# Hybrid attention and mixture-of-experts block on one core: projections as three rounded products, moved within the attention steps, and twenty products of constants in the head

## Chip, cores and metric

The kernel runs on one core of one Trainium2 chip. The metric is the device time of one execution in microseconds. The core has TensorE (PE, with its own queue of weight loads, PEld), VectorE (DVE), ScalarE (ACT), GpSimd (POOL) and the sequencer SyncE (SP), which only issues transfers here.

## What is computed

One decoder layer over 512 tokens of width 1024, all in float32. Cut to what matters here:

```python
mod = silu(c) @ w_ada + b_ada                 # six vectors: shift, scale, gate for attention and for ffn
h = rms_norm(x, g_attn) * (1 + scale_a) + shift_a
proj = h @ w_in                               # 3072 columns: dq dk dv | sq sk sv, 512 each
a_out = diff_attention(rms_norm(dq), rms_norm(dk), dv)     # 4 heads, two 64-wide maps each, ALiBi
b_out = stick_breaking_attention(sq, sk, sv)               # 8 heads of 64
x = x + gate_a * (concat(a_out, b_out) @ w_out)
h = rms_norm(x, g_ffn) * (1 + scale_f) + shift_f
x = x + gate_f * hier_moe(h)                  # best of 4 groups, best 2 of 8 experts in it, 32 experts
```

## The kernel before

The kernel is written by hand, one program per engine, with semaphores between them; within an engine the order is the program order, so a wait holds back all that stands behind it on that engine.

**Head.** SP loads x (2 MB), eight quarters of the shift and scale columns of w_ada (1 MB each) and then the first of six pieces of w_in (2 MB each, 512 columns; two places in the tile `stage`, so piece n is loaded once the last job of piece n-2 is done). ACT normalizes x, PE transposes it, DVE sums the w_ada quarters weighted with silu(c) (`first_sums`, line 799), PE adds the sums over partitions (`column_sums`, line 1242), DVE makes `mod`, and ACT writes hT, the modulated transposed input, in eight tiles k (line 590). POOL loads both gate biases (1 MB together, line 496), and from the middle of the scale sums on the remaining w_ada quarters (line 514).

**Projection jobs.** `plan_jobs` numbers the jobs: qk 0 to 7 (dq, dk), v 0 to 3 (dv), two gate jobs, then sq 0 to 3, sk 0 to 3, and four jobs v(n,1) (sv), with two `col` jobs (sums over partitions for the shift and scale of the ffn), `shift_router` and two more gate jobs among them. Job n writes PSUM bank n % 2 and waits until job n-2's result was read out. A job has eight k. The jobs qk 1 to 7 and v 0 to 3 run in `run_split`: weight and input are each split into a rounded part (hi) and a rest (lo), and three products of type float32r stand for one float32 product (line 1333). For them ACT rounds a chunk of 128 weight columns (`w_round`, line 598), DVE subtracts (`w_rest`, line 846), and hT is split the same way (lines 850, 853 on DVE, 506 on POOL). The other projection jobs run in `run` as float32 products (lines 1280 and 1285), which PE carries out as two instructions each. While the qk jobs run, ACT and DVE also norm dq and dk (lines 612 to 620, 874).

**Attention steps.** The loop over s runs on PE, ACT and DVE. Step s < 16 belongs to unit s (head s // 4, row block s % 4, width 128 to 512 columns). On PE before the change: `scores(s)` (line 1355), `probT_make(s-1)` (transposes, line 1369), `pv(s-2)` (line 1381), sometimes `fin_T` (line 1391), and last the projection parts of the step: two halves in steps 0 to 7, one in steps 8 to 15. On ACT: read out the jobs of step s-1, copy the transposes of unit s-1 (`probT_evac(s-1)`, line 661), exponentials of unit s (`exp_unit(s)`, line 653). On DVE: read out jobs of step s-1, `combine_unit(s-1)` (lines 934 to 938), `max_unit(s)` (lines 923, 927), then in steps 0 to 7 one w_ada quarter (lines 798, 799).

```python
for s in range(STEPS):                        # ACT, before
    if 1 <= s < DIFF_STEPS:
        for job in step_jobs.get(s - 1, ()):
            job_evac(job)
    if 1 <= s <= NT * DH:
        probT_evac(s - 1)
    if s < NT * DH:
        exp_unit(s)
```

Steps 16 on are stick-breaking attention, then the output projection (line 1474), routing, and 16 pairs of experts (lines 1582, 1601) whose 96 MB of weights SP loads into slots as they come free; the tiles hT, qkT, mixT, alibi, obuf, stage and val serve as those slots.

Of the kernel before, what the change touches and what calls it, by code (L numbers as in the profile page):

```python
# [5 lines left out]
F32 = mybir.dt.float32  # L6
# [7 lines left out]
P = 128  # L14
# [55 lines left out]


# [31 lines left out]
def hymba_block(nc, x, c, w_ada, b_ada, g_attn, w_in, q_norm_g, k_norm_g, lambda_q1, lambda_k1,  # L103
# [11 lines left out]
    with ExitStack() as ctx:  # L115
# [18 lines left out]
        xr = sb("xr", [P, NT, D])  # L134
        stage = placed_sb("stage", [P, 3, 4096])
        hT = sb("hT", [P, KD, T])
        qkT = placed_sb("qkT", [P, 16, T])
        val = sb("val", [P, NT, 1024])
        mixT = placed_sb("mixT", [P, KD, T])
# [3 lines left out]
        obuf = placed_sb("obuf", [P, 4, T])  # L143
# [13 lines left out]
        hT_hi = rounded("hT_hi", [P, KD, T], "qkT", 8 * T)  # L157
        hT_lo_parts = [rounded("hT_lo0", [P, 4, T], "mixT"), rounded("hT_lo1", [P, 4, T], "obuf")]
# [3 lines left out]
        def hT_lo(k):  # L162
            return hT_lo_parts[k // 4][:, k % 4, :]
# [88 lines left out]
        wr_ready = sem("wr_ready")  # L252
# [98 lines left out]

        def split_chunk(n):
# [4 lines left out]
            return raw[:, :, part], w_hi[:, :, part], lo[:, :, part], arrived, value  # L357
# [10 lines left out]
        def _(sp):  # L368
# [40 lines left out]
            sp.wait_ge(job_done, job_no[("v", 3, 1)] + 1)  # L409
            sp.wait_ge(ada_used, 16)  # L410
# [41 lines left out]
        def _(pool):  # L452
# [42 lines left out]
            for n, v in enumerate((GATE_A, GATE_F)):  # L495
                g.dma_start(gates[:, n, :], row(b_ada[:, v * D:(v + 1) * D])).then_inc(gate_bias_in, 16)

            for v in range(GATE_A, GATE_F + 1):
                for i in range(4):
                    n, dst, arrived, _ = quarter(v, i)  # L500
                    if n == 0:
                        pool.wait_ge(scale_used, KD // 2)
                    if n == 2:
                        for k in range(1, KD, 2):
                            pool.wait_ge(hT_hi_ready, k + 1)
                            g.tensor_tensor(hT_lo(k), hT[:, k, :], hT_hi[:, k, :].bitcast(F32),
# [7 lines left out]
                    g.dma_start(dst, ada_v[:, 2 * i:2 * i + 2, v * D:(v + 1) * D]).then_inc(arrived, 16)  # L514

            for w in range(2 * NT - 1):
# [46 lines left out]
        def _(act):  # L563
# [1098 lines left out]
```

## Time and profile before

| | us |
|---|---|
| median of 3 runs | 682.06 |
| lowest, highest | 679.41, 684.06 |
| profiled execution | 682.16 |
| its span, first to last instruction | 680.0 |
| PE busy in it | 561.3 (83%) |
| DVE, ACT, POOL busy | 275.7, 170.2, 82.2 |
| mean granted TensorE clock | 0.938 |

All rows below are of the profiled execution and start at its first instruction. "L1280 x16" means sixteen instructions of line 1280. A matmul's recorded duration overlaps the next one's; the distance from one start to the next is what it costs. In the chain of waits each piece is what the following one waited for.

### The profile page before, as it was taken

The numbers are of one execution on the slowest core, as the hardware profiler recorded it, in microseconds if no ns is written. First come the engines' busy times: TensorE is split into PE (matmuls) and PEld (weight loads), VectorE is DVE, ScalarE is ACT, GpSimd is POOL, SyncE is SP. The second block draws the span as 40 slices with busy tenths as digits, with TensorE's granted clock in tenths as the row PEclk, the third lists the DMA queues.
The fourth block names the chain that finished last, engine by engine and source line by source line (L and its number), as shares of the span: only waits on it lengthen the run. The fifth ranks groups of instructions, "written<-read, shape, count | busy, mean of one in ns | idle before, by whom it ended". The sixth has DMA issues, their size and how long they took to land.

```text
span 680.0 us, 7324 instructions
## 1 busy us (share of the span) xinstructions
PE 561.3 (83%) x2832; PEld 330.4 (49%) x2832; DVE 275.7 (41%) x474; ACT 170.2 (25%) x310; POOL 82.2 (12%) x98
## 2 busy tenths in 40 slices
PE   3379989999989899999999925988998898788740
PEld 2347768446455445665445613544554454344410
DVE  3866680553734455655012275222322232222005
ACT  7045541221222336786133210000000000000002
POOL 8331100000000000000021202111121112010000
PEclk9999999997998899999999955999999999889985
DMA  8984753537120007000751382899999999999719
GB/s 344 407 271 168 276 211 134 185 124 247 62 92 33 1 0 308 2 0 1 293 232 62 129 335 70 319 417 416 416 416 417 415 417 417 418 417 417 315 42 355
DMA packets 42384, 163.24 MB, mean 240 GB/s; under 512 B 7796, under 2 KB 7796, under 8 KB 34164
## 3 DMA queue, kind: packets, MB, share of 16 engines
q1 hardware_dynamic: 31972, 134.52, 49.6%
q0 software_dynamic: 9248, 26.23, 10.9%
q10 hardware_dynamic: 1136, 2.11, 0.8%
q8 instruction: 19, 0.31, 0.2%
q14 instruction: 9, 0.07, 0.0%
HBM read 158.64 MB, written 12.58 MB: 252 GB/s over the span
## 4 chain that ended last, share of the span: by engine, by line
PE 67%; DMA 14%; SPq 7%; DVE 7%; ACT 3%; issue 2%; POOLq 0%; DVEq 0%; ACTq 0%
PE banks L1582 11%; PE banks L1280 10%; PE banks L1474 8%; PE banks L1333 8%; PE banks L1601 6%; PE banks L1285 4%; DMA stage<-in_w_in_dram 4%; DMA stage<-in_w_dram 4%; DMA qkT<-in_w_dram 4%; PE banks L1426 3%; PE banks L1410 2%; PE banks L1570 2%; DMA stage<-pair_rows 2%; SPq L371 2%; PE banks L1355 1%
## 5 line engine op out<-in xcount | busy, mean ns | idle before, releaser
L1601 PE MATMUL banks<-stage,work 128*64 128x512 f32 x168 | 63.1, 638 | 10.0 <-ACT work L767 5.8
L1280 PE MATMUL banks<-hT,stage 128*128 128x512 f32 x144 | 66.4, 616 | 1.5 <-DMA stage<-in_w_in_dram 1.5
L1582 PE MATMUL banks<-qkT,work 128*64 128x256 f32 x272 | 63.6, 391 | 0.0
L765 ACT ACTIVATE work<-banks 128x256 f32<-128x256 f32 x16 | 6.1, 384 | 222.6 <-PE banks L1582 222.6
L1474 PE MATMUL banks<-stage,mixT 128*128 128x512 f32 x128 | 56.2, 594 | 0.0
L1185 DVE TENSOR_TENSOR work<-banks,gates 128x1024 f32<-128x1024 f32 x16 | 19.6, 1225 | 85.5 <-PE banks L1601 85.5
L1582 PE MATMUL banks<-hT,work 128*64 128x256 f32 x192 | 45.2, 394 | 2.6 <-DMA qkT<-in_w_dram 2.6
L799 DVE SCALAR_TENSOR_TENSOR mixT<-stage,small,mixT 128x1024 f32<-128x1024 f32 x35 | 44.9, 1282 | 3.5 <-DMA stage<-in_w_ada_dram 2.8
L1280 PEld LDWEIGHTS banks<-hT,stage 128*128 128x128 f32 x144 | 27.9, 199 | 34.0 <-issue 31.5
L1180 DVE TENSOR_TENSOR work<-work,banks 128x256 f32<-128x256 f32 x16 | 6.7, 421 | 88.3 <-ACT work L765 88.3
L534 POOL DMA_INDIRECT pair_rows<-work,tables x16 | 16.1, 1005 | 202.4 <-DVE work L1185 202.4
L1582 PEld LDWEIGHTS banks<-qkT,work 128*64 128x64 f32 x272 | 37.1, 140 | 5.9 <-issue 0.8
L1582 PE MATMUL banks<-mixT,work 128*64 128x256 f32 x160 | 36.0, 381 | 3.5 <-DMA obuf<-in_w_dram 2.4
L1474 PEld LDWEIGHTS banks<-stage,mixT 128*128 128x128 f32 x128 | 24.0, 190 | 28.9 <-issue 28.9
L1582 PE MATMUL banks<-stage,work 128*64 128x256 f32 x160 | 35.8, 381 | 0.0
L1582 PEld LDWEIGHTS banks<-hT,work 128*64 128x64 f32 x192 | 26.6, 142 | 18.9 <-issue 4.8
L1601 PEld LDWEIGHTS banks<-stage,work 128*64 128x64 f32 x168 | 17.9, 146 | 34.3 <-issue 28.0
L519 POOL TENSOR_TENSOR xr<-xr,obuf 128x512 f32<-128x512 f32 x7 | 8.8, 1266 | 191.1 <-DVE obuf L1023 191.1
L1285 PE MATMUL banks<-stage,hT 128*128 128x512 f32 x64 | 31.2, 634 | 0.0
L1582 PEld LDWEIGHTS banks<-mixT,work 128*64 128x64 f32 x160 | 21.3, 137 | 15.1 <-DMA obuf<-in_w_dram 3.3
L923 DVE CUSTOM_DVE_ANT_0 work<-banks,alibi 128x128 f32<-128x128 f32 (+3 forms) x32 | 14.4, 488 | 32.8 <-PE banks L1355 32.8
L514 POOL DMA_DIRECT2D stage<-in_w_ada_dram x16 | 11.5, 721 | 122.1 <-DVE mixT L799 122.1
(263 smaller groups left out, 1089.4 us busy)
## 6 DMA issues: line engine op xcount, KB each, us to landing
stage<-in_w_dram SPq DMA_DIRECT2D x31, 1024.0 KB, 20.5
qkT<-in_w_dram SPq DMA_DIRECT2D x23, 1024.0 KB, 20.9
stage<-in_w_ada_dram POOLq DMA_DIRECT2D x16, 1024.0 KB, 5.6
stage<-in_w_in_dram SPq DMA_DIRECT2D x6, 2048.0 KB, 10.1
hT<-in_w_dram SPq DMA_DIRECT2D x12, 1024.0 KB, 18.2
val<-in_w_dram SPq DMA_DIRECT2D x10, 1024.0 KB, 18.4
mixT<-in_w_dram SPq DMA_DIRECT2D x10, 1024.0 KB, 18.6
alibi<-in_w_dram SPq DMA_DIRECT2D x5, 1024.0 KB, 23.6
```

The costliest lines, as they stand in the source:

```text
L371: sp.dma_start(dst[i // 2][:, 2 * (i % 2):2 * (i % 2) + 2, :], ada_v[:, 2 * i:2 * i + 2, v * D:(v + 1) * D]).then_inc(first_in[4 * v + i], 16)
L534: g.indirect_dma_start(y_dram, bass.IndirectOffsetOnAxis(ap=tables[:, 1, q:q + 1], axis=0), ysb[:, r, :], None, bounds_check=2 * T - 1, oo ...
L799: return v.scalar_tensor_tensor(out=dst, in0=src, scalar=s, in1=dst, op0=ALU.mult, op1=ALU.add)
L923: ins = v.tensor_tensor_reduce(out=prob[:, u % 2, m, 0:W], in0=banks[:, 2 + 2 * (u % 2) + m, 0:W], in1=alibi[:, h, T - W:T], scale=1.0, sc ...
L1185: v.tensor_tensor(ysb[:, r, :], banks[:, 4 + 2 * r:6 + 2 * r, :].rearrange("p b k -> p (b k)"), gates[:, 1, :], ALU.mult).then_inc(ysb_rea ...
L1280: ins = mm(bank, w[:, k, ch * P:(ch + 1) * P], hT[:, k, :], start=(k == 0), stop=(k == KD - 1))
L1285: ins = mm(bank, hT[:, k, job[1] * P:(job[1] + 1) * P], w[:, k, :], start=(k == 0), stop=(k == KD - 1))
L1333: ins = mm(bank, still, moving, start=(k + m == 0), stop=(k == KD - 1 and m == 2))
L1426: ins = mm(zps[n % 2][:, o:o + W], still[:], part[:, n % 2, ZOFF[j]:ZOFF[j] + W], start=False, stop=True, skip_group_check=True)
L1474: ins = mm(banks[:, w % 5, :], mixT[:, k, t * P:(t + 1) * P], wv[:, k % 4, half * 512:(half + 1) * 512], start=(k == 0), stop=(k == KD - 1))
L1582: ins = mm(banks[half * C:(half + 1) * C, 2, up * F:(up + 1) * F], heT[:, r, k * P + half * C:k * P + (half + 1) * C], ws[2 * place + half ...
L1601: ins = mm(banks[half * C:(half + 1) * C, 4 + 2 * r + col, :], geT[:, fc * P + half * C:fc * P + (half + 1) * C], w2s[2 * place + half][:, ...
```

## The change

- All twelve float32 projection jobs and job qk 0 now run as three float32r products. ACT and DVE split chunks 12 to 23 of w_in for them: chunk 12 behind the head, chunk s+13 in step s up to step 5, then 19 and 20, 21 and 22, 23 in steps 6, 7 and 8. In each step this stands last, behind `exp_unit(s)` on ACT and behind the w_ada quarter on DVE.
- POOL splits chunk 0. Job qk 0 first makes its products with the rounded input, then those with the rest.
- The rounded input lies over x, whose tile is loaded again (2 MB) after the last projection; the rest lies over hT itself. DVE writes all eight rounded tiles before its four rests.
- The gate jobs of the head stand before v 0 to 3, no longer behind them. POOL's w_ada quarters also wait for piece 0 of w_in, and each gate bias is loaded behind its own quarters.
- On PE the projection parts of a step stand directly behind `scores(s)`, before `probT_make(s-1)`. Step 8 has no projection part, step 15 two; `col` 3 and `shift_router` are in step 8, the two late gate jobs in steps 12 and 14. The second eight w_ada quarters are summed in steps 0, 2, 4, 6, 8, 9, 10, 11.
- Before the column sums of the scale, once its last quarter is in, PE runs twenty bf16 products of constants (128x256) into an unused part of a bank.

```diff
-    head = [("qk", n) for n in range(8)] + [("v", t, 0) for t in range(NT)] + [("gate", 0, 0), ("gate", 0, 1)]
+    head = [("qk", n) for n in range(8)] + [("gate", 0, 0), ("gate", 0, 1)] + [("v", t, 0) for t in range(NT)]
...
-        for _ in range(2 if s < 8 else 1):
+        for _ in range({8: 0, 15: 2}.get(s, 2 if s < 8 else 1)):
             steps[s].append(halves.pop(0))
     steps[3].append((("col", 2), None))
-    steps[7].append((("col", 3), None))
-    steps[9] += [(("gate", 1, 0), None), (("shift_router",), None)]
-    steps[11].append((("gate", 1, 1), None))
+    steps[8] += [(("col", 3), None), (("shift_router",), None)]
+    steps[12].append((("gate", 1, 0), None))
+    steps[14].append((("gate", 1, 1), None))
...
+ADA_STEPS = (0, 2, 4, 6, 8, 9, 10, 11)
...
+        hT_hi = rounded("hT_hi", [P, KD, T], "xr")
+        hT_lo = rounded("hT_lo", [P, KD, T], "hT")
+        w_hi_spare = rounded("w_hi_spare", [P, KD, P], "work", 3072)
...
+        def split_at(s):
+            return {0: (13,), 6: (19, 20), 7: (21, 22), 8: (23,)}.get(s, (s + 13,) if s < 6 else ())
...
             sp.wait_ge(job_done, job_no[("v", 3, 1)] + 1)
+            sp.dma_start(xr[:], x_rows).then_inc(x_again, 16)
...
-            for n, v in enumerate((GATE_A, GATE_F)):
-                g.dma_start(gates[:, n, :], row(b_ada[:, v * D:(v + 1) * D])).then_inc(gate_bias_in, 16)
+            raw, hi, lo, arrived, value = split_chunk(0)
+            pool.wait_ge(arrived, value)
+            g.tensor_copy(hi, raw).then_inc(w0_hi, 1)
+            pool.wait_ge(w0_hi, 1)
+            g.tensor_tensor(lo, raw, hi.bitcast(F32), ALU.subtract).then_inc(w0_split, 1)
...
                     if n == 0:
                         pool.wait_ge(scale_used, KD // 2)
+                        pool.wait_ge(piece_in[0], 16)
...
                 act.wait_ge(arrived, value)
-                if n >= 4:
-                    act.wait_ge(job_done, n - 3)
+                if hi_before(n) is not None:
+                    act.wait_ge(job_done, job_no[chunk_job(hi_before(n))] + 1)
+                if n == 12:
+                    act.wait_ge(norm_done, 8)
                 a.activation(hi, raw, ACT.Copy).then_inc(w_hi_ready, 1)
...
             for job in head_jobs:
                 job_evac(job)
+            w_round(12)
...
                 if s < NT * DH:
                     exp_unit(s)
+                for n in split_at(s):
+                    w_round(n)
...
             for job in head_jobs:
                 job_evac(job)
+            w_rest(12)
...
-                if s < 8:
-                    ada_quarter(SCALE_F + s // 4, s % 4)
+                if s in ADA_STEPS:
+                    i = ADA_STEPS.index(s)
+                    ada_quarter(SCALE_F + i // 4, i % 4)
+                for n in split_at(s):
+                    w_rest(n)
...
             column_sums(0, shift_used)
+            pe.wait_ge(first_in[7], 16)
+            for _ in range(20):
+                mm(banks[:, 0, 256:512], ident_bf, consts[:, 5, :].bitcast(BF16), start=False, stop=True,
+                   skip_group_check=True)
             column_sums(1, scale_used).then_inc(col_a, 1)
...
+            def project(job, bank, ks):
+                c = IN_JOBS.index(job)
+                lo = w_lo_parts[:, c // 4 % 2, :].rearrange("p (k n) -> p k n", k=KD)
+                if job[0] == "v":
+                    pe.wait_ge(w_split, c // 4 * 4 + 3)
...
+                if c == 0:
+                    pe.wait_ge(w0_split, 1)
+                    for k in ks:
+                        pe.wait_ge(hT_hi_ready, k + 1)
+                        mm(bank, w_hi[:, k, part], hT_hi[:, k, :], start=(k == 0), stop=False)
+                        mm(bank, lo[:, k, part], hT_hi[:, k, :], start=False, stop=False)
                     pe.wait_ge(hT_lo_dve, KD // 2)
                     pe.wait_ge(hT_lo_pool, KD // 2)
+                    for k in ks:
+                        ins = mm(bank, w_hi[:, k, part], hT_lo[:, k, :], start=False, stop=(k == KD - 1))
+                    return ins
+                pe.wait_ge(w_split, c)
+                hi = chunk_hi(c)
+                for k in ks:
+                    mm(bank, hi[:, k, :], hT_hi[:, k, :], start=(k == 0), stop=False)
+                    mm(bank, hi[:, k, :], hT_lo[:, k, :], start=False, stop=False)
+                    ins = mm(bank, lo[:, k, part], hT_hi[:, k, :], start=False, stop=(k == KD - 1))
+                return ins
...
                 if s < NT * DH:
                     scores(s)
+                for job, part in step_parts.get(s, ()):
+                    run(job, part)
                 if 1 <= s <= NT * DH:
                     probT_make(s - 1)
                 if 2 <= s < DIFF_STEPS:
...
-                for job, part in step_parts.get(s, ()):
-                    run(job, part)
```

Here `IN_JOBS` lists the 24 projection jobs in the order of their chunks, so the job sq n has chunk 12 + n and sk n chunk 16 + n; `w_split` counts the finished `w_rest`.

## Rows read from the trace of the kernel before

**Rows 1.** The page's part 2, 40 slices of 17 us: busy tenths, GB/s.
```profile
PE   3379989999989899999999925988998898788740
...
GB/s 344 407 271 168 276 211 134 185 124 247 62 92 33 1 0 308 2 0 1 293 232 62 129 335 70 319 417 416 416 416 417 415 417 417 418 417 417 315 42 355
```

**Rows 2.** Chain of waits, 0 to 330: start us, us, what.
```profile
58.14 5.49 PE banks L1333 x24
...
94.78 3.51 DVE w_lo L846 x3
...
98.42 5.69 PE banks L1333 x24
...
121.34 1.81 PE banks L1290 x4
...
123.58 7.06 PE banks L1280 x16
...
131.53 6.87 PE banks L1280 x16
...
147.76 0.48 PE banks L1369 x3
...
155.56 3.58 PE banks L1295 x16
...
163.61 8.07 PE banks L1280 x16
...
213.90 3.44 PE banks L1285 x8
```

**Rows 3.** Who waited for whom, PE alone, 90 to 330: total us, times, longest.
```profile
PE banks L1369 <- DVE work L938: 6.4, 4, 2.2
```

**Rows 4.** Groups by line and shape, 0 to 330: busy us, mean ns, idle before.
```profile
L846 DVE TENSOR_TENSOR w_lo<-stage,w_hi 128x1024 fp32r<-128x1024 f32 x11 | 13.3, 1222 | 0.3
...
L598 ACT ACTIVATE w_hi<-stage 128x1024 fp32r<-128x1024 f32 x11 | 11.4, 1059 | 2.2 <-PE banks L1333 2.2
```

**Rows 5.** Timeline of DVE, 76 to 126: start us, us, instruction.
```profile
98.83 0.75 DVE L874 SCALAR_TENSOR_TENSOR qkT<-qkT,small,work 128x512 f32<-128x512 f32 x1 [0.56 <-ACT work L620]
99.50 2.60 DVE L799 SCALAR_TENSOR_TENSOR mixT<-stage,small,mixT 128x1024 f32<-128x1024 f32 x2
...
122.31 0.69 DVE L894 TENSOR_TENSOR gates<-banks,gates 128x512 f32<-128x512 f32 x1 [15.06 <-PE banks L1290]
```

**Rows 6.** Timeline of ACT, 138 to 166: copy of transposes, then exponentials of step 3.
```profile
148.28 0.49 ACT L661 ACTIVATE work<-banks 128x384 f32<-128x384 f32 x1 [0.94 <-PE banks L1369]
149.36 0.72 ACT L653 ACTIVATE work<-work,small 128x512 f32<-128x512 f32 x1 [0.59 <-DVE small L927]
...
150.69 0.18 ACT L653 ACTIVATION_READ_ACCUMULATOR work<-work,small 128x1 f32 x1
```

**Rows 7.** Timeline of all engines in the head, 0 to 60.
```profile
19.50 1.36 POOL L496 DMA_DIRECT2D gates<-in_b_ada_dram  x2
...
29.62 5.25 DVE L799 SCALAR_TENSOR_TENSOR mixT<-stage,small,mixT 128x1024 f32<-128x1024 f32 x4 [2.04 <-DMA stage<-in_w_ada_dram]
...
34.93 3.96 PE L1242 MATMUL banks<-consts,mixT 128*128 128x1 f32 x16 [8.76 <-DVE mixT L799]
...
39.50 5.47 ACT L590 ACTIVATE hT<-banks,small 128x512 f32<-128x512 f32 x8 [22.21 <-DVE small L840]
...
42.97 8.84 PE L1280 MATMUL banks<-hT,stage 128*128 128x512 f32 x16 [1.51 <-DMA stage<-in_w_in_dram]
...
44.58 1.64 DVE L853 TENSOR_TENSOR hT_lo<-hT,hT_hi 128x512 fp32r<-128x512 f32 x1
```

**Rows 8.** Windows: busy us (x) of PE, PEld, DVE, ACT, POOL; clock, DMA share, GB/s.
```profile
95.65:98.40 2.75, 0.57 (x2) 0.01 (x1) 2.63 (x3) 2.72 (x5) 0.11 (x1) 1.00 0.64 180
...
204.50:210.00 5.50, 5.43 (x14) 3.54 (x15) 1.62 (x10) 1.36 (x5) 0.00 (x0) 0.50 0.16 64
...
234.00:237.50 3.50, 3.42 (x12) 2.81 (x13) 1.43 (x10) 1.36 (x5) 0.00 (x0) 0.52 0.00 0
```

More of the change, by code:

```diff
@@ L356, in split_chunk, with chunk_job, hi_before @@
             part = slice((n % 4) * P, (n % 4 + 1) * P)
-            return raw[:, :, part], w_hi[:, :, part], lo[:, :, part], arrived, value
+            return raw[:, :, part], chunk_hi(n), lo[:, :, part], arrived, value
+        def split_at(s):
+            return {0: (13,), 6: (19, 20), 7: (21, 22), 8: (23,)}.get(s, (s + 13,) if s < 6 else ())
+        IN_JOBS = ([("qk", n) for n in range(8)] + [("v", t, 0) for t in range(NT)] + [("sq", n) for n in range(4)]
+                   + [("sk", n) for n in range(4)] + [("v", t, 1) for t in range(NT)])
+        def chunk_job(n):
+            return IN_JOBS[n // 4 * 4 + 3] if IN_JOBS[n][0] == "v" else IN_JOBS[n]
+        def hi_before(n):
+            return {12: None, 16: 12, 20: 8}.get(n, n - 4 if n >= 4 else None)
         IN_LAST = {0: ("qk", 3), 1: ("qk", 7), 2: ("v", 3, 0), 3: ("sq", 3), 4: ("sk", 3), 5: ("v", 3, 1)}
@@ L514, in _ @@
                     g.dma_start(dst, ada_v[:, 2 * i:2 * i + 2, v * D:(v + 1) * D]).then_inc(arrived, 16)
+                for u, vec in enumerate((GATE_A, GATE_F)):
+                    if v == vec:
+                        g.dma_start(gates[:, u, :], row(b_ada[:, v * D:(v + 1) * D])).then_inc(gate_bias_in, 16)
+            pool.wait_ge(x_again, 16)
             for w in range(2 * NT - 1):
@@ L1271, in run @@
                 kind = job[0]
[L1272 to L1285 removed]
+                if kind in ("qk", "sq", "sk", "v"):
+                    ins = project(job, bank, ks)
                 elif kind == "gate":
@@ L1310, in qk_norm @@
                 mm(banks[:, 2 + n % 2, :], halves, sqb[:, n % 2, :], start=True, stop=True).then_inc(norm_done, 1)
[L1312 to L1319 removed]
+            def project(job, bank, ks):
[3 more added lines that the diff above has]
+                    pe.wait_ge(w_split, c // 4 * 4 + 3)
+                    part = slice(job[1] * P, (job[1] + 1) * P)
+                    for k in ks:
+                        mm(bank, hT_hi[:, k, part], w_hi[:, k, :], start=(k == 0), stop=False)
+                        mm(bank, hT_hi[:, k, part], lo[:, k, :], start=False, stop=False)
+                        ins = mm(bank, hT_lo[:, k, part], w_hi[:, k, :], start=False, stop=(k == KD - 1))
+                    return ins
+                part = slice((c % 4) * P, (c % 4 + 1) * P)
+                if c == 0:
[4 more added lines that the diff above has]
+                        mm(bank, lo[:, k, part], hT_hi[:, k, :], start=False, stop=False)
@@ L1320, in run_split @@
                     pe.wait_ge(hT_lo_dve, KD // 2)
                     pe.wait_ge(hT_lo_pool, KD // 2)
-                lo = w_lo_parts[:, (2 if n >= 8 else n // 4) % 2, :].rearrange("p (k n) -> p k n", k=KD)
-                for k in range(KD):
-                    if job[0] == "qk":
-                        part = slice((n % 4) * P, (n % 4 + 1) * P)
-                        products = [(w_hi[:, k, part], hT_hi[:, k, :]), (w_hi[:, k, part], hT_lo(k)),
-                                    (lo[:, k, part], hT_hi[:, k, :])]
-                    else:
-                        part = slice(job[1] * P, (job[1] + 1) * P)
-                        products = [(hT_hi[:, k, part], w_hi[:, k, :]), (hT_hi[:, k, part], lo[:, k, :]),
-                                    (hT_lo(k)[:, part], w_hi[:, k, :])]
-                    for m, (still, moving) in enumerate(products):
-                        ins = mm(bank, still, moving, start=(k + m == 0), stop=(k == KD - 1 and m == 2))
@@ L1336, in _ @@
+                return ins
             for i, job in enumerate(head_jobs):
-                if i == 0 or job[0] == "gate":
-                    run(job)
-                else:
-                    run_split(job)
+                run(job)
                 if 1 <= i <= 8:
```

52 lines of the change are left out of this document (15 added, 37 removed).

## The prediction

> **What bounds the kernel now.** I first read the slices of the page [rows 1]: PE is busy nine tenths or more of nearly every slice from 50 to 390 us, and the later part of the kernel is triggered by PE's progress, so I take a shift at the end of attention to carry to the end one for one. Then the chain of waits from 43 to 260 us [rows 2], because the change lies there: nearly every piece is PE, one projection job after another. A float32 job is sixteen instructions in 6.87 us; a job of three rounded products is twenty-four in 5.49. Outside PE the chain has only the split at 94.78, just before v 0, and short waits of the transposes for DVE, 6.4 us in all [rows 3]. Last I looked at the granted clock around such waits [rows 8] and at the head [rows 7].
>
> **The plain saving.** Twelve jobs from 6.87 to 5.49 us: 12 x 1.38 = 16.6 us of PE work less [rows 2]. That is a gain only as far as PE stays what the chain follows. What each piece waits for in the new order decides that, so I go through it in order of time.
>
> **Head (to the start of qk 1).** Before, the scale sums end at 34.87, held up 2.04 us by a transfer, and qk 0 starts at 42.97 because piece 0 lands then [rows 7]. Without 1 MB of gate bias and 2 MB of quarters in front, at the 407 GB/s of that slice [rows 1], piece 0 lands about 7 us earlier and the scale sums end at 32.8 or before. The trace has no such filler products. A bound from below is the cheapest matmul spacing, 5.49 / 24 = 0.229 us for 512 columns, so 0.115 for 256: 2.3 us for twenty. From above the same at half clock, 4.6 us; before this point PE ran its column sums in 3.96 us, against 3.58 for the same sixteen later at full clock [rows 2, 7], so I take 4.5. They start when the last quarter is in: before by 32.2, as DVE ran its last four sums without a pause from 29.62, so now about 29.4; they end near 33.9: the column sums start about 1 us earlier than before, hT comes 1 us earlier (from 38.5, complete at 44). POOL's split of chunk 0 is not in the trace; at one to two DVE times of 1.22 for the copy and twice that for the subtraction [rows 4] it is 2.4 to 5 us after the piece, still at 40. Then the rests of hT are late: DVE starts its four only when all eight rounded tiles are written, 44.3, at 0.7 us alone or 1.64 beside POOL [rows 7], so they are done at 47 to 49.5, and the last eight products of qk 0 end at 49 to 51.5 against 51.8. Head: -1 (between -4 and +0.5).
>
> **v 0 to 3.** The move of the gate jobs takes 1.81 us from behind them [rows 2], into the wait before v 0. But v 0 is now two jobs behind gate 0, and shares its bank. DVE reads that gate out only behind the split of chunk 11 (ends 98.28), the norm of qk 6 (98.83), a w_ada quarter (99.50, 2.60) and the norm of qk 7 (0.75): 102.8, plus 0.69 for the gate itself [rows 2, 5] = 103.5. v 0 starts there and not at 98.42: +5.1. The norm product of qk 7, 0.9 us, moves before it: -0.9.
>
> **First step.** Chunk 12 is rounded by ACT only after the read-out of v 3: 0.5 + 1.0, then 1.22 on DVE and 0.2 of hand-over [rows 4]: sq 0 starts 3.0 us behind v 3, where it now takes 0.4 behind the gates. Together: 5.1 - 0.9 - 1.8 - 0.4 + 3.0 = +5.0 us for the start of sq 0.
>
> **Steps 0 to 8.** This is the step on which all hangs. ACT's order is probT_evac(s-1), exp_unit(s), w_round(s+13). The first waits for the transposes of unit s-1, and these now stand behind the projection job of step s. So the weights of the next job are split only after this job: job 5.49, transposes about 0.4 (three take 0.48), copy 0.4, exponentials of 0.85 (128 columns) to 1.5 us (512 columns, 149.36 to 150.87), w_round 1.06, w_rest 1.22, hand-over 0.2 [rows 2, 4, 6]. That is 9.6 to 10.3 us from job to job; PE's own work, job, scores, transposes and values, is some 7.1. Before it was 7.95, from 123.58 to 131.53 [rows 2]. DVE's quarter (2.6) is hidden: it runs under the 5.49 of the job. From the start of sq 0: 5.9 for step 0 (chunk 13 is ready in time), then 9.6, 10.05, 14.05 (column sums, 3.58, now before the transposes), 9.95, 9.6, 10.05, and from sk 3 to the first half of v(0,1) in step 9, past column sums, shift_router, a second pass through ACT and DVE and chunk 23, 17.6: 86.8 us. Before, the same stretch was 123.58 to 213.90 = 90.3. So -3.5, though eight jobs alone save 11.
>
> **Steps 9 to 16.** No split is left and PE is the longer side again. Before, seven halves of 3.44; now six of 2.75 and one whole: -2.1. The router job has moved away: -0.6. Two of the four waits of PE for DVE's probabilities stand here, each behind a gate job that DVE reads out first; DVE now has the gate before it is asked for the probabilities, and some 2.8 of the 6.4 us go [rows 3], with 0.9 for the half clock behind the second. But the job in step 15 stands before the transposes of unit 14, and unit 15's exponentials and combination (about 3.9 us) then run open, with 1 us under pv: +3.2. Sum -3.2. The second load of x, 2 MB, starts when transfers are nearly idle and is wanted 70 us later: 0, and at worst the 5 us that 2 MB take.
>
> **Clock.** So far -1 + 5.0 - 3.5 - 3.2 = -2.7 us. But the new waits leave PE idle 2.1 to 3.0 us in each of steps 1 to 7. After two of the waits of before the granted clock stood at 0.50 and 0.52 (the 1.2 GHz level) for 5.5 and 3.5 us, after the 2.2 us before v 0 it stayed at 1.00 [rows 8]; the job behind the column sums of step 3 took 8.07 instead of 6.87 and had started late as well [rows 2]. I count the half clock as sure after the open wait before v 0 (4.7 us, 1.7 lost), after the column sums of step 3 and in step 8 (1.7 each), and in half of the six shorter waits (3 x 1.3): +9.0. Bounds: +4 and +20.
>
> The Trainium skill says against this change (TensorE: Matmul & The Clock Gate, "HAM oscillation — how this bites in real kernels") that bursts of matmuls with waits between them can start each burst cold. By that rule all nine waits cost, and the sum is that of the second rival below; the trace so far agrees with it in two waits and not in the one before v 0.
>
> Sum: -2.7 + 9.0 = +6.3. The terms are of the profiled execution, 682.16 us around a span of 680.0, which is within 0.1 of the median of 682.06. Forecast 688.
>
> **Rivals.**
> - The split chain as worked out, with some half clock: 683 to 693, likeliest 688. Chance 0.45.
> - The clock holds in the short waits as it did before v 0: +1.7 x 2 or less, 677 to 684, likeliest 680. For it: PE still does transposes, values and scores in each gap. Against: waits of at most 2.2 us [rows 3] have cost the clock [rows 8]. Chance 0.25.
> - The clock falls at every job: -2.7 plus nine times 1.7 to 2.2 = +12.6 to +17, and if the low clock slows the transposes too, +20: 695 to 702. For it: the waits come once per job, each as long as those of before that ended at 0.50. Against: the 5.49 us of dense work in each step. Chance 0.18.
> - The other side: PE stays what the chain follows, because the next chunk's split is done before PE gets to its job. Then steps 0 to 8 take 8 x 7.1 plus 7.9 of column sums and router work, some 65 to 70 instead of 86.8, and the result is 682 - 20 = 662 to 672. It decides if the chain from the transposes to the split, 4.2 to 4.8 us, falls under the 1.7 us that PE has there. Against: each of its durations has its row. The same change could come from a head in which the fillers keep the clock up, worth 2 us more. Chance 0.12.
> - The fillers do nothing for the clock: column sums of 3.6 us and a pause follow them, and after such a stretch it stood at half in step 3. That is in my sum.
>
> **Numbers.** Predicted 688; range 674 to 700, which leaves out most of the fast case and the end of the slow one. About 1% (6.8 us) is what this measurement can tell from no change: below 675.3 lies the fast case, 0.14. Above 688.9 lie 0.4 of the likeliest and all of the third case: 0.38. Between them 0.48.
>
> **What the profile will show.** Right: v 0 starts 5 us behind the last w_lo; each w_hi of steps 1 to 5 starts right behind the exponentials of its step, and the job behind waits for DVE's w_lo; jobs start 9.6 to 10.3 us apart in steps 1, 2, 4, 5, 6; granted clock under 0.9 in some of the steps. The forecast is wrong if PE has no wait for w_lo in the steps, if the waits are there but the clock stays at 1.00, or if the head ends more than 4 us earlier.

## The result

| | before | after |
|---|---|---|
| median, us | 683.04 (4 runs) | 703.56 (4 runs) |
| lowest, highest | 679.41, 684.06 | 701.44, 705.45 |
| span of the profiled execution | 680.0 | 703.2 |
| mean granted TensorE clock | 0.938 | 0.902 |

After over before is 1.0309, 95% interval 1.0255 to 1.0363. The forecast was 688, range 674 to 700: the direction was right, the size was not. Two experiments below had one execution over 1.5% above their fastest (680.53 us in e6_early; 677.78 in e8_comb, which is its profiled one), and their medians are of the other three.

First the page of the changed kernel, part 2 (40 slices of 17.6 us). Beside [rows 1], PE has a hole in slice 6, before v 0, and holes from slice 8 to 16.

```profile
PE   3669979887878898999999952899889988878740
...
PEclk9979998998787997699999975799999998999985
```

Where PE waited, between 100 and 345 us of the changed kernel (total us, times, longest); [rows 3] answers to the second line.

```profile
PE banks L1369 <- DVE w_lo L879: 18.0, 7, 2.8
PE banks L1404 <- DVE work L972: 4.7, 4, 2.4
PE banks L1349 <- DVE gates L927: 4.5, 1, 4.5
PE banks L1349 <- ACT val L657: 1.5, 2, 0.9
PE banks L1349 <- DVE small L931: 1.4, 1, 1.4
```

Line 879 is the split on DVE, 972 the end of combine_unit, 927 the read-out of a gate job. The first and the third line are the two waits that the prediction had worked out. The chain of waits of the changed kernel shows the first one whole (start us, us, what), between the transposes of unit 0 and the job of step 2:

```profile
145.24 0.12 PE banks L1404
...
145.56 1.08 ACT work L684 x4
146.64 0.95 ACT w_hi L628
...
147.62 1.24 DVE w_lo L879
...
148.99 0.77 PE banks L1369
149.75 0.43 PE banks L1370
```

Transposes, exponentials, rounding, subtraction, and only then the job. This chain repeats in steps 2 to 7, with waits of 1.9 to 2.8 us (the seventh wait of that line, 2.6 us, is that for chunk 12 before sq 0). In step 2 the job's products are at first 0.43 us apart, not 0.23, since the clock fell in the wait; in steps 5 and 7 it did so too, in steps 3 and 6 it stayed at 1.00, and in step 4 it was down already from the column sums.

The wait before v 0, on DVE's timeline (start us, us; line 907 norms qk, 832 sums w_ada); beside [rows 5], the gates now stand between the norms and v 0:

```profile
96.61 3.50 DVE L879 TENSOR_TENSOR w_lo<-stage,w_hi 128x1024 fp32r<-128x1024 f32 x3
100.65 0.75 DVE L907 SCALAR_TENSOR_TENSOR qkT<-qkT,small,work 128x512 f32<-128x512 f32 x1 [0.55 <-ACT work L650]
101.32 2.60 DVE L832 SCALAR_TENSOR_TENSOR mixT<-stage,small,mixT 128x1024 f32<-128x1024 f32 x2
103.96 0.75 DVE L907 SCALAR_TENSOR_TENSOR qkT<-qkT,small,work 128x512 f32<-128x512 f32 x1
104.62 1.28 DVE L927 TENSOR_TENSOR gates<-banks,gates 128x512 f32<-128x512 f32 x2
```

To place the loss I took, from PE's timeline of each profile, the start of six marks in us: job qk 2, v 0, sq 0, the projection part of step 9, the first stick-breaking scores (step 16), the first product of the output projection; and the span. The experiments' profiles are listed with them, for their sections.

| | qk 2 | v 0 | sq 0 | step 9 | step 16 | output proj. | span |
|---|---|---|---|---|---|---|---|
| before | 57.6 | 98.4 | 123.5 | 213.7 | 257.9 | 319.0 | 680.0 |
| after | 59.4 | 105.4 | 133.2 | 228.6 | 274.7 | 342.6 | 703.2 |
| e1_order | 59.0 | 105.0 | 132.8 | 206.7 | 250.0 | 312.1 | 668.9 |
| e2_gates | 59.4 | 100.3 | 127.1 | 221.0 | 267.5 | 334.8 | 691.5 |
| e3_both | 59.2 | 100.0 | 128.4 | 203.0 | 246.1 | 307.1 | 665.7 |
| e4_warm | 59.2 | 105.1 | 130.1 | 221.9 | 267.4 | 328.5 | 688.5 |
| e5_nofill | 57.7 | 98.6 | 127.0 | 201.6 | 244.5 | 305.6 | 663.9 |
| e6_early | 57.6 | 103.6 | 131.4 | 204.0 | 248.7 | 310.8 | 668.0 |
| e7_old | 57.7 | 98.6 | 123.7 | 210.2 | 258.4 | 326.2 | 684.2 |
| e8_comb | 60.7 | 101.5 | 126.6 | 201.6 | 246.6 | 314.2 | 675.7 |
| e9_best | 60.7 | 101.5 | 126.7 | 200.9 | 241.3 | 302.3 | 658.8 |
| e10_s16 | 59.2 | 105.2 | 131.6 | 228.6 | 273.6 | 334.7 | 694.4 |
| e11_ada | 60.3 | 106.3 | 133.0 | 228.7 | 273.4 | 335.4 | 691.9 |
| e12_nohl | 59.0 | 99.8 | 126.5 | 201.0 | 241.6 | 302.6 | 659.2 |

Stage by stage the changed kernel gave away 1.8 (head), 5.2 (to v 0), 2.7 (v jobs and first split), 5.2 (steps 0 to 8), 1.9 (steps 9 to 15), 6.8 (stick-breaking) and got 0.4 back behind: 23.2 us between the two spans. The largest single one lies in the stick-breaking stage, in which the change alters no work of the engines; only the second load of x now runs beside it. These windows (busy us (x) of PE, PEld, DVE, ACT, POOL; clock; DMA share; GB/s) show the first 16.4 us of it, first after, then before:

```profile
274.70:291.10 16.40, 16.40 (x48) 10.16 (x48) 5.99 (x9) 6.72 (x8) 0.00 (x0) 0.50 0.82 335
```

```profile
257.90:274.30 16.40, 15.43 (x78) 9.90 (x78) 9.82 (x15) 12.15 (x18) 0.00 (x0) 1.00 0.82 321
```

48 products against 78 in the same time, at a clock of 0.50 against 1.00 (the 1.2 and the 2.4 GHz level). PE's timeline of the changed kernel shows how it fell into this: the open wait in step 16, and half speed from the first transposes behind it.

```profile
269.27 0.63 PE L1426 MATMUL banks<-consts,obuf 128*128 128x128 f32 x4 [0.23 <-ACT work L692]
272.34 1.11 PE L1404 MATMUL banks<-consts,work 128*128 128x128 f32 x4 [2.44 <-DVE work L972]
273.25 1.48 PE L1416 MATMUL banks<-val,work 128*128 128x128 f32 x6
274.67 2.93 PE L1445 MATMUL banks<-qkT 64*128 64x384 f32 x6
```

### The profile page after: what moved, and what is told of

Read it like the earlier page. It is cut to its first block, busy times and chain, and to the rows that moved or that the text cites. A ratio compares the mean times of both kernels' runs of the same rounds, so it can differ in the third digit from the quotient of the medians.

```text
span 703.2 us, 7612 instructions
## 1 busy us (share of the span) xinstructions
PE 566.1 (81%) x2956; PEld 365.8 (52%) x2956; DVE 289.4 (41%) x486; ACT 179.6 (26%) x322; POOL 86.0 (12%) x100
## 3 DMA queue, kind: packets, MB, share of 16 engines
q10 hardware_dynamic: 1136, 2.11, 0.8%
## 4 chain that ended last, share of the span: by engine, by line
PE 62%; DVE 10%; SPq 10%; DMA 9%; ACT 6%; issue 3%; POOLq 0%; DVEq 0%; ACTq 0%
PE banks L1617 11%; PE banks L1509 8%; PE banks L1636 6%; PE banks L1369 5%; PE banks L1370 4%; PE banks L1371 4%; DMA qkT<-in_w_dram 3%; PE banks L1461 3%; PE banks L1445 3%; DMA stage<-in_w_ada_dram 3%; SPq L418 2%; PE banks L1349 2%; PE banks L1605 2%; PE banks L1350 2%; PE banks L1351 2%
## 5 line engine op out<-in xcount | busy, mean ns | idle before, releaser
L1369 PE MATMUL banks<-hT_hi,w_hi 128*128 128x512 f32 x104 | 46.1, 443 | 12.7 <-DVE w_lo L879 12.7
L1371 PE MATMUL banks<-hT_hi,w_lo 128*128 128x512 f32 x120 | 49.6, 413 | 0.0
L1370 PE MATMUL banks<-hT_lo,w_hi 128*128 128x512 f32 x104 | 42.8, 411 | 0.0
L879 DVE TENSOR_TENSOR w_lo<-stage,w_hi 128x1024 fp32r<-128x1024 f32 x21 | 25.4, 1223 | 37.1 <-ACT w_hi L628 36.8
L1349 PE MATMUL banks<-w_hi,hT_hi 128*128 128x512 f32 x64 | 27.1, 423 | 7.4 <-DVE gates L927 4.5
L1369 PEld LDWEIGHTS banks<-hT_hi,w_hi 128*128 128x128 f32 x104 | 21.1, 203 | 21.9 <-issue 17.6
## 6 DMA issues: line engine op xcount, KB each, us to landing
hT<-in_w_dram SPq DMA_DIRECT2D x12, 1024.0 KB, 17.6
```

Of the source, the lines that this page charges most:

```text
L879: v.tensor_tensor(lo, raw, hi.bitcast(F32), ALU.subtract).then_inc(w_split, 1)
L1349: mm(bank, hT_hi[:, k, part], w_hi[:, k, :], start=(k == 0), stop=False)
L1369: mm(bank, hi[:, k, :], hT_hi[:, k, :], start=(k == 0), stop=False)
L1370: mm(bank, hi[:, k, :], hT_lo[:, k, :], start=False, stop=False)
L1371: ins = mm(bank, lo[:, k, part], hT_hi[:, k, :], start=False, stop=(k == KD - 1))
```

## Experiments

**Undoing the placements.** The theory: two placements make the loss, the projection parts before the transposes (with the split behind them on ACT) and the gates before v 0; the clock makes it larger. The rival: ACT and DVE are overloaded by the splits, wherever things stand. e1_order undoes the first, e2_gates the second, e3_both both.

```diff
@@ e1_order and e3_both, PE's loop over s @@
                 if s < NT * DH:
                     scores(s)
-                for job, part in step_parts.get(s, ()):
-                    run(job, part)
...
                     if s == fin_step(f) + 2:
                         fin_T(f)
+                for job, part in step_parts.get(s, ()):
+                    run(job, part)
```

```diff
@@ e2_gates and e3_both, plan_jobs @@
-    head = [("qk", n) for n in range(8)] + [("gate", 0, 0), ("gate", 0, 1)] + [("v", t, 0) for t in range(NT)]
+    head = [("qk", n) for n in range(8)] + [("v", t, 0) for t in range(NT)] + [("gate", 0, 0), ("gate", 0, 1)]
```

> The changed kernel with one thing undone: on PE the projection parts of a step stand behind the transposes and value products again, as before the change; ACT and DVE still split the next chunk last in their step. Theory A (the split of the next chunk waits, by way of the transposes, for the job of its own step): jobs come 7 to 8 us apart in steps 0 to 7 and no longer 9.6 to 12, the open wait in step 16 and the half clock behind it go; 22 us for the steps and 8 for the stick-breaking stage, so about 673 to 676. Rival B (ACT and DVE have too much work in each step with the splits, wherever the job stands): jobs stay 9.5 us or more apart, 690 to 700.

Measured 671.74 us, 0.984 of before (0.9817 to 0.9862): 32 us faster than the changed kernel, and a little faster than theory A said (673 to 676). Steps 0 to 8 took 73.9 us instead of 95.4 (table). PE's waits in e1_order, 100 to 320 us:

```profile
PE banks L1404 <- DVE work L972: 8.6, 9, 1.4
PE banks L1349 <- DVE gates L927: 4.5, 1, 4.5
PE banks L1369 <- DVE w_lo L879: 2.6, 1, 2.6
```

The wait for the split has gone from seven times to one, that of chunk 12. Jobs start 6.3 to 7.5 us apart in steps 0 to 3 and 7.2 to 9.3 in steps 4 to 7. DVE now makes PE wait nine times for the probabilities, 8.6 us in all, where it was four times and 6.4 us before [rows 3]: rival B has that much truth.

> The changed kernel with the two gate jobs of the head behind v 0 to 3 again. Theory A (v 0 waits for DVE's read-out of gate 0, which stands behind a quarter and two norms, and the wait costs the clock as well): v 0 starts 2.7 us or so behind qk 7 instead of 9.7, less 5.1 us of wait and 3 of half clock, plus 2.7 for the gate and norm products behind or between the v jobs: 697 to 699. Rival B (v 0 would wait as long for the split of chunk 11): 703 to 706.

Measured 694.02 us, 1.0169 of before (1.0143 to 1.0196), 9.5 us faster than the changed kernel where 5 to 7 had been expected (697 to 699). Up to the output projection the table shows 7.8 us: v 0 5.1 earlier, and 1.0 and 1.5 more by sq 0 and step 9. The remaining 3.9 us of the spans lie behind the output projection, where the change alters nothing. They go with the clock: some 70 us into that part, in the routing, it falls to 0.50 in every profile, and the first expert products behind it run at half speed until it comes back. The windows of this stretch, the changed kernel and then e2_gates:

```profile
411.80:449.30 37.50, 15.96 (x84) 13.01 (x86) 20.53 (x75) 3.12 (x4) 4.09 (x4) 0.50 0.58 218
406.50:437.20 30.70, 10.08 (x56) 8.32 (x58) 19.62 (x74) 1.70 (x3) 4.09 (x4) 0.50 0.59 221
```

The stretch at half clock lasts 37.5 us in the kernel before, the changed one and e8_comb (output projection to the end: 360.6 to 361.5 us), 34.1 in e3_both, e4_warm, e5_nofill, e7_old and e10_s16 (358.0 to 360.0), and 30.7 in the other six (356.5 to 357.2). No experiment touches this, so that the clock is the cause is read from the traces and not tested; and some 4 us of a difference between two profiles can come from here, whatever was changed.

> Both undone: projection parts behind the value products, gate jobs behind v 0 to 3. Everything else of the change stays: twelve jobs more as three rounded products, the splits in the steps, chunk 0 on POOL, x loaded twice, the filler products. If the two placements are the whole loss and the rounded products are worth their 16.6 us: 666 to 671, faster than the kernel before. If the rounded products bring nothing because ACT and DVE then set the pace: 680 or more.

Measured 667.31 us, 0.9765 of before (0.9743 to 0.9787), within the 666 to 671 of the first theory. That is 15.4 us under the kernel before of the same runs (682.68), near the 16.6 that the rounded products save, with the other parts of the change still in it. The two placements together are 36 us, less than the 32 and 9.5 us that each gave alone.

**Only the clock.** e4_warm leaves every wait for another engine where it is and keeps PE busy in it; e10_s16 does so at one place.

```diff
+            def keep_warm(bank, count):
+                for _ in range(count):
+                    mm(bank[:, 0:256], ident_bf, consts[:, 5, :].bitcast(BF16), start=True, stop=True)
...
+                if c >= 12 and ks[0] == 0:
+                    keep_warm(bank, 20)
                 pe.wait_ge(w_split, c)
...
+                if job == ("v", 0, 0):
+                    keep_warm(banks[:, 4, :], 40)
                 run(job)
...
+                if s == NT * DH:
+                    pe.wait_ge(max_ready, NT * DH - 1)
+                    keep_warm(banks[:, 2, :], 20)
                 if 1 <= s <= NT * DH:
                     probT_make(s - 1)
```

> The changed kernel, its order untouched, with more bf16 products of constants while PE waits: 40 before v 0, 20 before each of the jobs sq and sk, 20 before the transposes of unit 15. The waits stay, only TensorE's granted clock should stay up. If the half clock is the larger part of the miss (3 us behind v 0, about 8 in the steps, about 7 in the stick-breaking stage, whose clock stood at 0.50 for 20 us): 686 to 692. If the waits alone carry it: 701 to 705.

Measured 688.94 us, 1.0081 of before (1.006 to 1.0102): 14.6 us of the 20.5 are gone with the waits still there. By stage against the changed kernel: v jobs 2.8, steps 0 to 8 3.6, stick-breaking 6.8. This is a net figure: where PE had no wait the added products delay it (sq 1 starts 8.4 us behind sq 0, not 6.3), and behind the column sums of steps 3 and 8 the clock still fell.

e10_s16 has only the last of the three pieces.

> The changed kernel with only twenty filler products before the transposes of unit 15, where PE waits for the probabilities 2.4 us. In the changed kernel the granted clock fell there and stood at 0.50 for 20 us of stick-breaking attention. Theory A (this one wait costs about 8 us through the clock, since sparse work behind it does not bring the clock back): 694 to 698. Rival B (the stick-breaking stage is longer for another reason, such as the 2 MB load of x beside the expert weights): 701 to 705.

Measured 695.33 us, 1.0182 of before (1.0147 to 1.0218): 8.2 us for twenty products at one place. The window that answers to the two above:

```profile
273.60:290.00 16.40, 15.43 (x78) 9.86 (x77) 9.79 (x15) 12.13 (x18) 0.00 (x0) 1.00 0.90 365
```

78 products again, while DMA moves more than in the changed kernel: the second load of x does not slow this stage. That the clock stays up is not owed to the twenty products for certain, as e11_ada below shows.

**The chain broken the other way.** e6_early keeps PE's order and moves the split on ACT and DVE.

```diff
@@ ACT, start of step s @@
+                for n in split_at(s):
+                    w_round(n)
                 if 1 <= s <= NT * DH:
                     probT_evac(s - 1)
                 if s < NT * DH:
                     exp_unit(s)
-                for n in split_at(s):
-                    w_round(n)
@@ DVE, between combine_unit(s - 1) and max_unit(s) @@
+                for n in split_at(s):
+                    w_rest(n)
@@ DVE, behind the w_ada quarter @@
-                for n in split_at(s):
-                    w_rest(n)
```

> The changed kernel with PE's order untouched; ACT rounds the next chunk at the start of a step, ahead of the copy of the transposes, and DVE subtracts it ahead of its maxima. So the split no longer waits for the job of its own step, although this job still stands before the transposes. Theory A (the split behind the transposes is what makes the jobs 9.6 to 12 us apart): jobs about 7.2 us apart in steps 0 to 7, steps 0 to 8 shorter by 20 us with the clock's part, the waits before v 0 and in step 16 as they were: 677 to 684. Rival B (projection jobs ahead of the transposes delay the softmax chain itself): still over 9 us apart, 695 or more.

Measured 672.41 us, 0.9844 of before (0.9808 to 0.988), below theory A's range. Steps 0 to 8 took 72.6 us, even less than with PE's order undone, so in these steps the job's place before the transposes does no harm by itself. PE's waits in e6_early, 100 to 330 us:

```profile
PE banks L1349 <- DVE gates L927: 4.5, 1, 4.5
PE banks L1404 <- DVE work L972: 3.6, 2, 2.4
PE banks L1369 <- DVE w_lo L879: 2.6, 1, 2.6
```

One wait for the split, that of chunk 12, and two for probabilities, one of them the open one of step 16 (2.4). Behind this one the clock stayed at 1.00 for over 8 us, and stick-breaking took 62.1 us instead of 67.9. That, 1.8 us in the head and 3.4 behind the output projection (see e2_gates) are why the profiled execution lies so far below the range.

**The order alone.** e7_old is the kernel before with only PE's parts moved.

```diff
-    steps[9] += [(("gate", 1, 0), None), (("shift_router",), None)]
+    steps[9].append((("gate", 1, 0), None))
+    steps[10].append((("shift_router",), None))
...
                     scores(s)
+                for job, part in step_parts.get(s, ()):
+                    run(job, part)
...
                         fin_T(f)
-                for job, part in step_parts.get(s, ()):
-                    run(job, part)
```

> The kernel before, with float32 jobs and no splits in the steps, and with one part of the change: the projection parts of a step directly behind the scores, before the transposes (shift_router moves from step 9 to step 10, which the new order needs). Theory A (the order costs only through the split behind the transposes, and at the end of step 15): PE's waits for DVE's probabilities, 6.4 us, and most half clock of steps 4 to 12 go, the open wait in step 16 and its clock come: 678 to 686. Rival B (the order itself stretches every step): 690 or more.

Measured 691.05 us, 1.0113 of before (1.0064 to 1.0162; 686.29 to 694.25), outside the range of A and, by the number, in that of B. By the marks of its profile B fails in steps 0 to 8, which took 86.5 us against 90.2 before. In steps 9 to 15 the order does cost: 48.2 us against 44.2, with the open wait of 2.4 us and with PE waiting 2.0 us for DVE to read out a gate job and 1.3 for ACT to read out a v job. Together that is 258.4 against 257.9 before; then stick-breaking took 67.8 us against 61.1. Its window has the same 48 products at 0.50 as the changed kernel:

```profile
258.40:274.80 16.40, 16.40 (x48) 10.12 (x48) 5.99 (x9) 6.72 (x8) 0.00 (x0) 0.50 0.51 209
```

I had priced this clock at too little again. The profiled execution is the fastest of the four (686.29); the others took up to 8 us more, and no trace shows where.

**The filler products of the head.** e5_nofill is e3_both without them.

> As e3_both (both placements undone, 667.3 us), and without the twenty products of constants before the column sums. In the changed kernel's head they end at 33.4, one us behind the last scale sum (32.4), and TensorE's granted clock has fallen to half before job qk 0 starts. Theory A (they only delay the column sums, and keep no clock for qk 0): 1 us faster, 665.5 to 667. Rival B (they do help, in the column sums or behind them): 668 to 670.

Measured 666.82 us, 0.9765 of before (0.9745 to 0.9785), against 667.31: no difference that these runs can tell, though it lies in theory A's range. On the timeline of the changed kernel the fillers delay the column sums, as the last scale sum was ready at 32.4:

```profile
29.53 3.99 PE L1293 MATMUL banks<-consts 128*128 128x256 bf16 x20 [3.41 <-DMA stage<-in_w_ada_dram]
33.36 3.86 PE L1279 MATMUL banks<-consts,mixT 128*128 128x1 f32 x16
...
49.95 3.69 PE L1364 MATMUL banks<-hT_lo,w_hi 128*128 128x512 f32 x8 [2.95 <-DVE hT_lo L886]
```

and the clock is at half when hT is ready (windows of 2 us):

```profile
36.00:38.00 2.00, 1.22 (x6) 1.13 (x5) 0.61 (x3) 0.00 (x0) 1.91 (x2) 0.58 0.14 11
38.00:40.00 2.00, 0.40 (x2) 0.41 (x3) 1.08 (x2) 1.24 (x2) 2.00 (x3) 0.50 0.45 85
```

In e5_nofill the last eight products of qk 0 came behind the same wait of 2.95 us at full clock and took 2.11 us, not 3.69. That is no merit of leaving the fillers out: e6_early has them, and its qk 2 started just as early, at 57.6.

**Quarters of w_ada.** e11_ada changes one tuple of the changed kernel.

```diff
-ADA_STEPS = (0, 2, 4, 6, 8, 9, 10, 11)
+ADA_STEPS = (0, 1, 2, 3, 4, 5, 6, 8)
```

> The changed kernel with one thing changed: the second eight quarters of w_ada in steps 0 to 6 and 8 instead of 0, 2, 4, 6, 8, 9, 10, 11. Theory A (the quarters in steps 9 to 11 stand before the probabilities on DVE and make PE wait 0.8 and 1.1 us there; in steps 1, 3 and 5 they hide under the wait for the split): 700 to 702. Rival B (they add to the chain in the early steps): 704 to 708.

Measured 693.9 us, 1.0167 of before (1.0131 to 1.0202), 9.7 us faster and not 1.5 to 3.5. PE's wait for probabilities fell from 4.7 us (4 times) to 3.2 (2 times), as A says, and step 9 to 16 is 1.4 us shorter. The rest is again clock: stick-breaking took 62.0 us instead of 67.9, and the part behind the output projection 356.5 instead of 360.6. PE waited the same 2.44 us in step 16, with nothing to do in it, and the clock did not fall; it fell later in the stage, for 3.4 us:

```profile
273.40:277.30 3.90, 3.90 (x22) 2.31 (x21) 0.00 (x0) 1.63 (x3) 0.00 (x0) 1.00 1.02 418
281.00:284.40 3.40, 3.40 (x14) 3.30 (x15) 3.33 (x6) 1.27 (x1) 0.00 (x0) 0.52 1.02 424
```

So the open wait is not enough to lose the clock. Over all profiles: with that wait open (2.44 to 2.48 us) stick-breaking took 67.2 to 67.9 us in four kernels (the changed one, e2_gates, e7_old, e8_comb) and 62.1 in two (e6_early, e11_ada); with the wait filled 61.1 in both (e4_warm, e10_s16), and with no wait there 61.0 to 62.1 in six. What decides between 67.9 and 62.1 is not shown. The four executions of e11_ada lie within 1.2 us of each other and those of the changed kernel within 4, so in these two it is not a toss at every execution; in e6_early, whose executions run from 669.73 to 680.53 us, it may be.

**A version that beats both.** e8_comb, e9_best and e12_nohl build on e5_nofill.

```diff
@@ all three: chunk 12 during the v jobs @@
             for job in head_jobs:
                 job_evac(job)
-            w_round(12)
+                if job == ("v", 0, 0):
+                    w_round(12)
...
+            w_rest(12)
             for job in head_jobs:
                 job_evac(job)
-            w_rest(12)
@@ e8_comb and e9_best, DVE: rests in turn with the rounded tiles @@
                 v.tensor_copy(hT_hi[:, k, :], hT[:, k, :]).then_inc(hT_hi_ready, 1)
-            for k in range(0, KD, 2):
-                dve.wait_ge(hT_hi_ready, k + 1)
-                v.tensor_tensor(hT_lo[:, k, :], hT[:, k, :], hT_hi[:, k, :].bitcast(F32),
-                                ALU.subtract).then_inc(hT_lo_dve, 1)
+                if k % 2 == 0:
+                    dve.wait_ge(hT_hi_ready, k + 1)
+                    v.tensor_tensor(hT_lo[:, k, :], hT[:, k, :], hT_hi[:, k, :].bitcast(F32),
+                                    ALU.subtract).then_inc(hT_lo_dve, 1)
@@ quarters and late gates: e8_comb @@
+ADA_STEPS = (0, 2, 4, 6, 8, 10, 12, 14)
+    steps[15] += [(("gate", 1, 0), None), (("gate", 1, 1), None)]
@@ quarters and late gates: e9_best and e12_nohl @@
+ADA_STEPS = (0, 1, 2, 3, 4, 5, 6, 8)
+    steps[10].append((("gate", 1, 0), None))
+    steps[12].append((("gate", 1, 1), None))
```

> A combination: e5_nofill (both placements undone, no filler products), and DVE makes the rest of hT in turn with the rounded tiles, chunk 12 is split while the v jobs run, and the second eight quarters of w_ada are summed in every second step up to 14 with both late gate jobs in step 15. If DVE sets the pace of steps 8 to 12 in e3_both because four quarters stand in a row there: 3 to 5 us less there, 1.5 for chunk 12, 1 to 2 in the head, 659 to 663. If PE sets it: 664 to 666.

Measured 666.27 us, 0.9753 of before (0.972 to 0.9786), above the range given; three executions took 663.75 to 668.2 us, the profiled one 677.78. In this one PE waits 2.48 us before step 16, and the clock stood at half for 17 us behind that; whether the others have this too was not seen. So the combination gains nothing for certain over e5_nofill.

> As e5_nofill (both placements undone, no filler products, 666.8 us), with three more moves: chunk 12 is split while the v jobs run, DVE makes the rest of hT in turn with the rounded tiles, and the second eight quarters of w_ada are summed in steps 0 to 6 and 8, with the late gate jobs in steps 10 and 12, so that steps 9 to 15 have no quarter before the probabilities. If DVE sets the pace of steps 8 to 12 in e5_nofill (4 quarters of 2.6 us in a row; step 9 to the end of step 15 took 43 us there, PE's own work is some 37): 4 us less there, 1.5 for chunk 12 and 1 to 2 in the head, 659 to 662. If the early steps give it back, since each now has a quarter and a split on DVE: 665 to 668.

Measured 662.76 us, 0.9711 of before (0.9682 to 0.9739), just above the range given. Step 9 to step 16 took 40.4 us against 42.9 in e5_nofill, the v jobs with the first split 25.2 against 28.4; the head lost 3.0. The three moves were not tried one by one.

> As e9_best (662.8 us), but DVE writes all eight rounded tiles of hT before its four rests, as the change has it. In the profile of e9_best job qk 2 started at 60.7, in e5_nofill, which has the change's order, at 57.7: with the rests in turn the rounded tiles came later, the first products of qk 0 ran out to 49 us and the half clock fell on qk 1. If that is the cause: 1 to 3 us faster than e9_best, 660 to 662. If the 3 us were the clock of one execution: 662 to 664.

Measured 662.0 us, 0.9685 of before (0.9658 to 0.9712): the best of all by its median, and not to be told from e9_best. qk 2 started at 59.0, between the two others, so whether the order of the rests matters stays open. It is 21 us under the kernel before and 42 under the changed one.

## The prediction, point by point

- **Rounded products, 16.6 us.** Right as a saving of work, and nearly reached in e3_both (15.4). In the changed kernel the work saved turned into waiting, as forecast.
- **Wait before v 0, +5.1.** Measured +5.2 for the stretch from qk 2; the sequence on DVE is the one worked out from [rows 5].
- **First split, 3.0 us behind v 3.** It is in the profile (the job sq 0 starts at 133.2). With half clock over the start of the v jobs this stretch took 2.7 us more than before, where -0.1 and 1.7 of clock had been counted: 1.1 short.
- **Steps 0 to 8.** The mechanism was right: e1_order and e6_early break it at two different ends, and both shorten the stretch by over 21 us. The sum was 86.8 us plus 7.3 of clock (two sure, three of six), 94.1; measured 95.4 against 90.2 before. Even the count was met: the clock fell in three of the six short waits. Job starts were 9.5 to 12.2 us apart where no column sums lay between, up to 2 us over the range where the clock had fallen. What is missing lies between sk 3 and step 9: 20.7 us, against 17.6 and 1.7 of clock.
- **Steps 9 to 16, -3.2 forecast, +1.9 measured.** A step that failed, by 5 us. "No split is left and PE is the longer side again" overlooked what the new w_ada quarters in steps 9, 10 and 11 do on DVE, between the maxima and the probabilities: PE waited 0.8 and 1.1 us behind the first two, and e11_ada took those waits away. It also overlooked that PE now reaches the next job before ACT, behind the exponentials, has read out the last one: waits of 0.6 and 0.9. The open wait in step 16 was forecast, and so was its cause; half clock between it and the first scores took 1.1 us more (2.33 us against 1.26 in e10_s16).
- **Clock, +9.0 forecast, some 14.6 measured (e4_warm, net).** This is the step that put the result outside the range. I priced each wait by the job behind it and stopped there. At the open wait of step 16 I counted the wait, +3.2 (it was 2.4), and no clock at all, though shorter waits had cost it in my own rows; and the assumption that a shift at the end of attention carries to the end "one for one" left no place for it. In the changed kernel it cost some 8 us (8.2 in e10_s16), the price of five of the other waits. With it and the 5 us above, the sum of +6.3 becomes about +19.5, close to the 20.5 measured. That it was lost here was in part chance: behind the same wait e6_early and e11_ada lost none, and e11_ada, at 693.9 us, would have been within the range. The term should have been a range from nothing to some 8 us.
- **Head, -1 forecast, +1.8 measured (+2.2 at qk 1).** The last eight products of qk 0 were to end at 49 to 51.5; they started at 49.95 and ended at 53.6. The rounded tiles were all written at 46.2, not 44.3, as DVE took 0.88 us for each of the last six and not 0.43, and the rests at 49.9, not 47 to 49.5 (four at the 1.64 us beside POOL would have given 50.9, so that bound was drawn too low). The products then took 3.69 us at half clock, and qk 1 began at half clock too. This wait, 2.95 us, had been named ("the rests of hT are late") and not put into the clock term.
- **Bounds and chances.** +20 was the upper bound given for the clock, but the range stopped at 700, where that bound alone led to 699 and a miss elsewhere had no room. Above 688.9 the shares named (0.4 of 0.45, and 0.18) make 0.36, not 0.38. The case "the clock falls at every job" (695 to 702) was nearest, and its mechanism is not what happened: the clock fell in half of the short waits, and then for 20 us behind the last.
- **The fillers of the head** gave no time, as forecast.
- **The Trainium skill** (TensorE: Matmul & The Clock Gate, "HAM oscillation — how this bites in real kernels") had spoken against the change, from a kernel with waits of about 3 to 5 us. The traces agree in part: of the nine waits of 1.9 to 4.5 us before which the clock of the changed kernel was up, it was at half behind six, and at 1.00 behind three (2.56, 2.75 and 1.91 us). Its case, 695 to 702, had been given a chance of 0.18.

## To carry to other kernels

A split, a cast or a load that a later matmul needs belongs on its engine's queue ahead of whatever that queue waits for from the matmuls of the same step; before moving work on one engine, read what the other engines' next instruction waits for. Price a new PE wait by two terms, the wait and the clock behind it, and give the second a range by the stage that follows: in the projection jobs here the clock was back before the job's end, while in stick-breaking it stayed down for some 17 to 20 us in four kernels. The lower end of that range is nothing, since the same wait cost no clock in two others. Where a wait can't be removed, a run of cheap products that fits into it is worth trying: with it stick-breaking stayed at full clock in both kernels that had it. The same products ahead of the head's column sums gave nothing.

## What was not expected of the hardware

- The granted clock stayed at 0.50 for some 20 us in the stick-breaking stage while PE was recorded busy all the time (16.40 of 16.40 us), in the changed kernel and in e7_old. In e11_ada, behind the same wait of 2.44 us, it did not fall, and in e10_s16, with the wait filled, it never fell in this stage.
- The half-clock stretch of the routing lasted 30.7, 34.1 or 37.5 us, and the part behind the output projection took 356.5 to 361.5 us with it, in kernels that do not differ there.
- Twenty products of 256 columns in bf16 took 3.99 us in the head of the changed kernel and 2.36 before sq 0 in e4_warm, at a clock of 1.00 (0.20 and 0.12 us each in the mean). Sixteen one-column products behind the former (3.86 us) took hardly less than in the kernel before (3.96), and behind them the clock was at half.
- POOL rounded 128x1024 elements in 1.04 us, less than I had allowed, and subtracted them in 2.35.
